# Expert routing with bf16 ranks and per-slot tables, raw rows gathered, and gated sums added to the outputs in DRAM behind each expert

## What is computed

```
def moe_ffn(x, w_r, wg, wu, wd):          # x is rmsnorm(residual, g_ffn)
    xt = x.reshape(-1, D)
    logits = jnp.dot(xt, w_r, preferred_element_type=F32)
    top_v, top_i = lax.top_k(logits, TOP_K)            # 2 of 8
    w = jax.nn.softmax(top_v, axis=-1)
    gates = jnp.einsum('tk,tke->te', w, jax.nn.one_hot(top_i, N_EXPERTS, dtype=F32))
    for e in range(N_EXPERTS):
        h = jax.nn.silu(xt @ wg[e]) * (xt @ wu[e])     # 1024 -> 3584
        y = y + gates[:, e:e + 1] * jnp.dot(h, wd[e])  # 3584 -> 1024
...
    x = x + ffn(rmsnorm(x, g_ffn))
```

## Time and profile before

| | |
|---|---|
| median of three runs | 1643.97 us (1643.64 to 1647.16) |
| the profiled execution's own time | 1651.6 us |
| its span, first to last instruction | 1649.8 us, mean granted TensorE clock 0.978 |
| busy, share of span | PE 96%, DVE 76%, ACT 60%, POOL 11% |
| router logits start on PE | 621.5 us from the span's start |
| first expert matmul | 652.3 us |
| last expert matmul ends | 1625.2 us |

### The profile page before, as it was taken

One profiled execution on the slowest core, in us unless ns is written; L12 is line 12 of the kernel. 1 busy time (PEld: TensorE's weight loads), 2 busy tenths in 40 slices (PEclk: granted clock), 3 DMA queues, 4 the chain that ended last, 5 costly groups with the idle time before them and its releaser, 6 DMA issues.

```text
span 1649.8 us, 21672 instructions
## 1 busy us (share of the span) xinstructions
PE 1582.9 (96%) x8463; PEld 1358.9 (82%) x8463; DVE 1247.7 (76%) x1262; ACT 994.8 (60%) x1068; POOL 177.1 (11%) x224
## 2 busy tenths in 40 slices
PE   6999999999999996999999999999999999999994
PEld 5988899999998895888888888888888888888883
DVE  4766666663476656888888888888888888888884
ACT  3554533333455343777777777777777777777772
POOL 4802320000150222000000000000000000000001
PEclk9999999999999996999999999999999999999997
DMA  5532595444443208999999999999999999999983
GB/s 154 145 102 78 106 325 165 148 166 141 134 130 106 78 30 296 356 363 354 389 369 358 388 368 367 387 367 361 387 370 362 386 369 366 384 362 370 386 333 108
DMA packets 230242, 450.03 MB, mean 273 GB/s; under 512 B 10240, under 2 KB 72524, under 8 KB 230140
## 3 DMA queue, kind: packets, MB, share of 16 engines
q1 hardware_dynamic: 214944, 420.64, 71.9%
q10 hardware_dynamic: 11132, 17.05, 2.9%
q0 software_dynamic: 4064, 10.96, 2.1%
HBM read 431.14 MB, written 17.47 MB: 272 GB/s over the span
## 4 chain that ended last, share of the span: by engine, by line
PE 90%; DVE 3%; DMA 3%; ACT 2%; POOL 1%; issue 1%; ACTq 0%; POOLq 0%; DVEq 0%
PE bank L1769 30%; PE bank L2215 13%; PE bank L2216 13%; PE bank L2220 13%; PE bank L2226 6%; PE bank L2235 6%; PE bank L2229 6%; PE bank L1772 2%; PE bank L2244 1%; DMA ring<-ffn_w_up 1%; ACT cut_hi L800 1%; DVE cut_lo L1177 1%; DMA xhat<-x_sample 1%; POOL acc L622 1%; DMA raw<-expert_rows,pos 1%
## 5 line engine op out<-in xcount | busy, mean ns | idle before, releaser
L1681 DVE TENSOR_TENSOR split_lo<-raw,split_hi 128x2048 fp32r<-128x2048 f32 x336 | 768.1, 2291 | 128.5 <-ACT split_hi L1098 127.9
L1098 ACT CAST split_hi<-raw 128x2048 fp32r<-128x2048 f32 x336 | 640.5, 1910 | 264.1 <-PE bank L2220 167.1
L2215 PE MATMUL bank<-split_hi,xgT_hi 128*128 128x512 f32 x896 | 359.3, 401 | 3.8 <-DVE xgT_lo L1705 3.8
L2216 PE MATMUL bank<-split_hi,xgT_lo 128*128 128x512 f32 x896 | 356.0, 397 | 0.0
L1177 DVE TENSOR_TENSOR cut_lo<-ring,cut_hi 128x1024 fp32r<-128x1024 f32 x124 | 153.5, 1240 | 135.0 <-ACT cut_hi L800 134.9
L800 ACT CAST cut_hi<-ring 128x1024 fp32r<-128x1024 f32 x124 | 129.6, 1048 | 206.7 <-PE bank L1769 191.9
L1769 PE MATMUL bank<-xT_hi,cut_hi 128*128 128x320 f32 x752 | 245.0, 326 | 5.5 <-DVE xT_lo L1191 2.2
L2220 PE MATMUL bank<-split_lo,xgT_hi 128*128 128x512 f32 x896 | 246.0, 396 | 0.0
L1769 PE MATMUL bank<-xT_hi,cut_lo 128*128 128x320 f32 x752 | 236.9, 315 | 0.0
L1769 PE MATMUL bank<-xT_lo,cut_hi 128*128 128x320 f32 x752 | 236.7, 315 | 0.0
L2215 PEld LDWEIGHTS bank<-split_hi,xgT_hi 128*128 128x128 f32 x896 | 169.2, 189 | 43.3 <-DVE xgT_lo L1705 4.2
(11 more groups left out here) (260 smaller groups left out, 1582.1 us busy)
## 6 DMA issues: line engine op xcount, KB each, us to landing
raw<-moe_w_gate SPq DMA_DIRECT2D x112, 1024.0 KB, 8.3
raw<-moe_w_up SPq DMA_DIRECT2D x112, 1024.0 KB, 8.1
raw<-moe_w_down SPq DMA_DIRECT2D x112, 1024.0 KB, 5.4
ring<-w_in SPq DMA_DIRECT2D x16, 1024.0 KB, 5.3
ring<-ffn_w_gate SPq DMA_DIRECT2D x11, 1024.0 KB, 6.6
ring<-ffn_w_up SPq DMA_DIRECT2D x11, 1024.0 KB, 5.4
ring<-ffn_w_down SPq DMA_DIRECT2D x10, 1024.0 KB, 5.1
ring<-w_out SPq DMA_DIRECT2D x8, 1024.0 KB, 5.1
```

Of the source, the lines that this page charges most:

```text
L1098: return nc.scalar.copy(split_hi[:, i % SR, :], raw[:, (i % PR) * PIECE:(i % PR + 1) * PIECE]).then_inc(hi_ready, 1)
L1681: V.tensor_tensor(split_lo[:, i % SR, :], raw[:, (i % PR) * PIECE:(i % PR + 1) * PIECE], split_hi[:, i % SR, :].bitcast(F32), ALU.subtract ...
L2215: TE.matmul(o, xgT_hi[:, kk, :], hi[:, c], start=kk == 0, stop=False)
L2216: TE.matmul(o, xgT_lo[:, kk, :], hi[:, c], start=False, stop=False)
```

## The change

1. Residual rows: ACT makes all six copies to `x`, PE makes the logits before the last x_rows, and POOL writes the unscaled rows `x` to `hx`. The reciprocal root of each token goes into a table instead.
2. Ranks: the top 2 are taken from unscaled logits; the ranks and counts are bf16 products.
3. Tables: `tag` holds 8 bf16 columns for each token and expert: token number (2), reciprocal root in three parts, gate in three parts. `G` against `tag` gives, by slot, token, root and gate (`slots`): for the first 128 slots of all experts before the expert stage (`idxA`, 24 matmuls), for the other 256 slots within the first expert (`late_members` on DVE at pieces 6 to 13, `late_tokens` on PE, 6 matmuls ahead of each of pieces 7 to 14, `idxB`).
4. Expert stage: the silu takes the root as its scale, `hm` takes it as a factor, `y_copy` takes the gate.
5. Outputs: POOL writes `x` to the outputs at the start of the expert stage, and behind each expert adds `ye` to the output rows by two indirect accumulating DMAs (prompt and stream rows; slots without a token point out of bounds and are dropped). `ybuf`, its zeros, the final gathers, the six DVE sums and the last stores are gone.
6. Weights: the seven first pieces are loaded as soon as their part of SBUF is free, the first four of them before the end of the output projection. ACT splits the first three before the exponential of the gates, and DVE makes their rests after `xg_lo`. ACT's fourth split waits for `idx_ready`.

```diff
@@ SP: first pieces @@
-                    sp.wait_ge(lo_ready, first + (i + 1))
+                    if begin and i < PR:
+                        if i == 0:
+                            sp.wait_ge(rope_ready, 6 * DEPTH)
+                            sp.wait_ge(RT.full, RT.filled(("tok", "va", 1, 2)))
+                        elif i <= RING:
+                            sp.wait_ge(cut_lo_ready, LAST_CUT[len(UNITS) - RING + i - 1] + 1)
+                        elif i == RING + 1:
+                            R, job = norm_end(3, KB - 1)
+                            sp.wait_ge(R.full, R.filled(job))
+                    else:
+                        sp.wait_ge(lo_ready, first + (i + 1))
@@ POOL @@
+            for t, (t0, rows) in enumerate(TILES):
+                pool.wait_ge(RS.free, RS.emptied(("xk", t, 0)))
+                pool.wait_ge(RC.free, RC.emptied(("xk", t, 1)))
+                pool.dma_start(hx[t0:t0 + rows, :], x[0:rows, t, :]).then_inc(hx_out, 16)
             for t, (t0, rows) in enumerate(TILES):
                 pool.wait_ge(rows_sq, t + 1)
                 rsqrt(rs_slot(1, "end", t), rows, D, 1)
...
+            def add_rows(n):
+
+                pool.wait_ge(rows_out, n * 32 + 32)
+                nc.gpsimd.tensor_copy(isc_p[:, 0:1], idx_p[:, bass.ds(n, 1)]).then_inc(isc_ready, 1)
+                nc.gpsimd.tensor_copy(isc_s[:, 0:1], idx_s[:, bass.ds(n, 1)]).then_inc(isc_ready, 1)
+                pool.wait_ge(isc_ready, n * 2 + 2)
+                pool.wait_ge(y_free, n + 2)
+                nc.gpsimd.tensor_copy(mark[:], idx[0:1, bass.ds(n, 1)])
+                pool.indirect_dma_start(out=y_p[0], out_offset=bass.IndirectOffsetOnAxis(ap=isc_p[:, 0:1], axis=0), in_=ye[:], in_offset=None,
+                                        bounds_check=SEQ - 1, oob_is_err=False, compute_op=ALU.add).then_inc(rows_out, 16)
+                pool.indirect_dma_start(out=y_s[0], out_offset=bass.IndirectOffsetOnAxis(ap=isc_s[:, 0:1], axis=0), in_=ye[:], in_offset=None,
+                                        bounds_check=DEC - 1, oob_is_err=False, compute_op=ALU.add).then_inc(rows_out, 16)
@@ ACT @@
-            act.wait_ge(pairs_ready, 1)
-            pairs = act.value_load(npair[0:1, 0:1], min_val=NE // 2, max_val=NE // 2 * MAXB)
...
-                nc.scalar.copy(ye[:, 0:512], banks[6][:])
-                nc.scalar.copy(ye[:, 512:1024], banks[7][:]).then_inc(y_free, 1)
-                act.wait_ge(y_free, ip * 2 + (h + 2))
-                act.dma_start(ybuf[bass.ds(ip * (2 * P) + h * P, P), :], ye[:]).then_inc(ye_out, 16)
+                nc.scalar.activation(ye[:, 0:512], banks[6][:], ACT.Copy, scale=now_w[:, h % 2, 1:2])
+                nc.scalar.activation(ye[:, 512:1024], banks[7][:], ACT.Copy, scale=now_w[:, h % 2, 1:2]).then_inc(y_free, 1)
...
+            act.wait_ge(idx_ready, 1)
             experts(2 * STRAIGHT, 0, SR)
@@ DVE @@
+            def late_members(e):
+
+                if e >= 2:
+                    dve.wait_ge(G2_used, e - 1)
+                for t, (t0, rows) in enumerate(TILES):
+                    last = V.tensor_scalar(G2[0:rows, e % 2, t], C("slot", rows)[:, P:MAXB * P], rankm[0:rows, t, e:e + 1], None, ALU.is_equal)
+                last.then_inc(G2_ready, 1)
...
             xg_lo(0, 0)
+            for i in range(SR):
+                dve.wait_ge(hi_ready, i + 1)
+                piece_lo(i)
+            slots(RD, ("idxA",), 0, NE)
...
-                        V.tensor_tensor(hm[:, m % 2, :], hs[:, m % 2, :], banks[2 + m % 2][:], ALU.mult).then_inc(u_free, 1)
+                        V.scalar_tensor_tensor(out=hm[:, m % 2, :], in0=banks[2 + m % 2][:], scalar=now_w[:, h % 2, 0:1], in1=hs[:, m % 2, :],
+                                               op0=ALU.mult, op1=ALU.mult).then_inc(u_free, 1)
```

More of the change, by code:

```diff
@@ L139 @@
 STRAIGHT = NE // 2 - 1
+PSLOT = [6] + [(len(UNITS) + j) % RING for j in range(RING)] + [3, 4, 5]
+AWAY = 100000.0
 HT_AT = [4 * _j + 11 for _j in range(FC - 1)] + [4 * FC + 7]
@@ new lines, in _, with slots @@
+            step(V.tensor_tensor(gatew[:], gatew[:], gatew2[:], ALU.add))
+            in_parts(gatew, 5, rest, lambda a: a[:]).then_inc(tag_ready, 1)
+            def slots(R, job, a, n):
+                dve.wait_ge(R.full, R.filled(job))
+                c = R.bank(job)[:, 0:8 * n].rearrange("p (n c) -> p n c", c=8)
+                f = slice(a, a + n)
+                V.tensor_reduce(place[:, f], c[:, :, 0:2], AX_X, ALU.add)
+                for w in range(2):
+                    last = V.tensor_reduce(slot_w[:, f, w], c[:, :, 2 + 3 * w:5 + 3 * w], AX_X, ALU.add)
+                last.then_inc(R.free, 1)
+                dve.wait_ge(R.free, R.emptied(job))
+                V.tensor_scalar(idx[:, f], place[:, f], -1.0, 0.0, ALU.add, ALU.max)
+                step(V.tensor_scalar(away[:, f], place[:, f], 1.0, AWAY, ALU.is_lt, ALU.mult))
+                step(V.scalar_tensor_tensor(out=spot[:, f], in0=place[:, f], scalar=-1.0, in1=away[:, f], op0=ALU.add, op1=ALU.add))
+                step(V.tensor_copy(idx_p[:, f], spot[:, f]))
+                step(V.tensor_scalar(away[:, f], place[:, f], float(SEQ + 1), AWAY, ALU.is_lt, ALU.mult))
+                step(V.scalar_tensor_tensor(out=spot[:, f], in0=place[:, f], scalar=-float(SEQ + 1), in1=away[:, f], op0=ALU.add, op1=ALU.add))
+                V.tensor_copy(idx_s[:, f], spot[:, f]).then_inc(idx_ready, 1)
@@ L1728, in experts @@
                     h, q = divmod(i, NP)
+                    if done and 6 <= i < 6 + NE:
+                        late_members(i - 6)
+                    if done and i == 8 + NE:
+                        slots(RO, ("idxB",), NE, (MAXB - 1) * NE)
                     dve.wait_ge(hi_ready, ip * (2 * NP) + (i + 1))
@@ L2149, in _ @@
             for t, (t0, rows) in enumerate(TILES):
-                last = mm(b, C("ones", rows), M[0:rows, t, :], t == 0, t == NT - 1)
+                last = mm(b, ones_bf[0:rows], M_bf[0:rows, t, :], t == 0, t == NT - 1)
             last.then_inc(RT.full, 1)
+            x_rows(RC, 2, 1)
             tb = [banks[4], banks[5]]
@@ L2205, in experts @@
                     if q == 4 * FC:
+                        if first and h == 0:
+                            pe.wait_ge(RO.free, RO.count)
+                            pe.wait_ge(RD.free, RD.count)
                         pe.wait_ge(y_free, ip * 2 + (h + 1))
```

314 lines of the change are left out of this document (160 added, 154 removed).

## The result

| | runs | median us | lowest to highest | profiled execution: span, clock |
|---|---|---|---|---|
| before, same chip | 4 | 1645.57 | 1643.64 to 1647.21 | 1649.8, 0.978 |
| changed | 4 | 1616.21 | 1613.73 to 1621.87 | 1615.8, 0.983 |

The ratio is 0.9823, 95% interval 0.9805 to 0.9840: 29.4 us faster, where 13.9 were predicted and the range ended at 1623.5. The direction is right and the size is not.

The account below looks back on a forecast made before the run. PE was taken to bound the expert stage (busy 247.69 of 247.70 us, full clock). Beginning -3.0, first expert +5.4 and end -16.3 sum to -13.9, from 1643.97 to 1630.0 us; 8-in-10 range 1623.5 to 1637.

Parts of the forecast that it names:

- Stage pace: Expert stage: PE sets the time, with 12 matmuls a piece and pieces of 2.90 us each.
- later experts 121.5 us as before: Expert stage after the first expert: each expert's time stays at 121.5 us, a sign to look for.
- Beginning of the stage: Last residual to first expert matmul: logits, ranks, gather, gates and tables come earlier, 3.0 us less.
- The five stations: Stage beginning, shifted by 3.4 us: gather issued 632.8, exponential 637.0, `tag` 639.3, tables 641.4, first matmul 645.9.
- First expert: First expert of the stage: stalls, late matmuls and late comparisons add 5.4 us, bounds 2.3 to 8.
- The stalls: First expert: PE waits as ACT's fourth split waits for the first table, and at later rests; 2.0 us.
- The late tables: First expert: late comparisons and matmuls hold pieces at 3.2 us, 3.2 us in all, plus 0.2 at the second table.
- The end: After the last matmul: two accumulating DMAs replace store, gathers, sums and output stores, 16.3 us less (11.8 to 18.7).
- the adds land late: Rival at the end: last add takes 9.6 us to land, end gain 11.7, total 1634.6; chance 0.09.
- Costed at nothing: Zeros' removal, earlier weight loads, each expert's adds, and root and gate as scales: taken to change no time.

Follow-up runs that it names:

- b_layout: Kernel before with 512 bytes of padding ahead of lamt and 160 ahead of xg, giving the changed kernel's operand addresses modulo 1024: 1624.43 us, ratio 0.9871.
- a_pad32: Changed kernel with 32 bytes of padding per partition ahead of xg: 1639.39 us, ratio 0.9948 to the kernel before.
- the two measurements by themselves: No kernel, only float32r matmul blocks with swept operand offsets, first 512 columns, then 512 and 320: 512 columns 226.7 ns at offsets 0 and 256.
- a_zeros: Changed kernel with the 8 MB store of zeros put back into layer 0's FFN, to a tensor nothing reads: 1616.78 us, ratio 0.9800.
- a_plain: Changed kernel with plain indirect stores in place of the accumulating ones, additions left out: 1615.78 us, ratio 0.9821.
- b_raworder: Kernel before with only the changed kernel's kind of raw slot order: 1647.63 us, ratio 0.9996.

## Why the prediction was off

- **"Stage pace" is the step that failed**: "2.90 us each", and "later experts 121.5 us as before". I priced every matmul of the stage at before's pace, since the code of the matmuls stays. The tiles' addresses do not, and they were part of the price: 121.4 us per expert before, 118.5 after. This is shown from both sides, by b_layout (before's code, 20.6 us less) and a_pad32 (the changed code with 32 bytes of padding, back at 0.9948), and on PE alone by the two measurements by themselves. It is the whole of the surprise, and more: without it the change would have fallen short of the forecast. No rival of the prediction had it, since all of them are about the stage's ends, its first expert or its transfers. At the old pace the change is still faster, as the mechanism said, but by some 8 us.
- **Beginning of the stage, -3.0: right.** -2.8 in the profiled pair, and -2.2 to -2.6 between the profiles with the later start (a_zeros and a_plain against b_raworder and b_layout). The five stations compared above came within about half a microsecond, the half clock in the stretch included, and the transposes did wait for the tables, as forecast. Two readings were off and cost nothing: the rows landed 4.8 us behind the gather's issue and not some 8, so they lay ready 4.4 us ahead of the transposes and not 0.5; and it was DVE's own `G` and casts that held `tag`, not the splits ahead of the exponential, though by 0.1 us only.
- **First expert, +5.4: right in kind, 0.9 too small, and closer than its terms.** Against b_layout it is 126.9 - 120.6 = 6.3 us. Two terms missed in opposite directions. The stalls, 2.0 in the sum, came to about 1.0: the fourth split did wait for the table (9.36 us of ACT's idle time ended on `idx_s`), but PE lost only 0.27 us by it, and 0.7 by the rests of pieces 5 to 7. The late tables, 3.4 in the sum, took 4.9: the comparisons cost DVE 0.26 us each start to start, as forecast (0.25), and DVE needs the 3.2 us per piece that it was given, but PE's own late matmuls add 0.6 us to a piece, at full clock, and not 0.4. So PE held the pieces and not DVE. The 0.4 us that are left lie in the first piece, at half clock, and behind the last late one.
- **The end, -16.3: mis-sized, -11.4 in the pair.** It took 13.2 us and not 8.3. `ye` is ready 1.37 us after the last matmul; the second add starts 2.8 us after it and not 2.1, since an accumulating issue takes 1.57 us and not the 0.94 of the earlier trace rows; the landing takes 4.9 us, as I took it (5); and behind the last landing lie 4.2 us that the sum had at nothing, 3.75 of them POOL's drain. The rival "the adds land late" had the size right by luck: it put the last landing at 9.6 us behind its issue, and it came at 4.9. What the additions cost is 2.8 us (a_plain), most of it inside the 5 us that the sum had allowed.
- **Costed at nothing: right.** The zeros (a_zeros: same time), the adds of each expert, the scales. DMA share was 1.03, and in the later experts no wait of PE shows.
- **The sum without the pace** is about -8 us by medians. The terms above give -2.8 + 6.3 - 11.4 = -7.9. The prediction had -13.9, so with the old addresses it would have been 6 us too optimistic, nearly all of it (4.9) in the end, and the addresses then hid that by giving 20.

The Trainium skill, TensorE: Matmul & The Clock Gate, section "Back-to-back issue gap", gives N/2.4 + 2.5 ns at full clock for an isolated matmul, 216 ns at 512 columns, and about 131 ns for a sustained stream of weight loads and matmuls. The runs here, with float32r and a weight load for each matmul, show 226.7 on average at best and up to 234.7 at other offsets, so that neither of the page's figures is reached at any offset.

## What to carry to other kernels

Where PE is the bound and the clock is full, compare the count of matmuls in an equal stretch of both kernels, not the busy time: a busy share of 100% hides a 3% change of pace. Before a change that adds or removes an SBUF tile is judged, pin the addresses of the matmuls' operands with padding, or try it with both placements; else the placement's share is credited to the code. For 512-column float32r matmuls put the moving and the stationary tile at the same address modulo 256 bytes: here padding alone won 20 us, more than the change's own code (some 8), and 32 bytes ahead of these tiles lost it again.

## What the chip showed that was not expected

The pace of a stream of 512-column float32r matmuls depends on the difference of its two operands' SBUF addresses: 226.7 ns at a multiple of 256 bytes, 228.9 at 64, 231 to 235 elsewhere, with patterns of two to eight matmuls that repeat, on PE alone. At 320 columns there is no such gain. An accumulating indirect store was issued in 1.57 us at the end of the kernel, against 0.98 for a plain one. And the span ended 2 to 4 us behind the last landing, on POOL's drain.
